# Reordering the entry of the block-product stage: two more banks, block sums on another engine, a convolution in another place

## The chip, the cores and the metric

The kernel runs on one core of one Trainium2 chip. The metric is device microseconds of one launch. A core has TensorE (PE, matrix products), VectorE (DVE), ScalarE (ACT), GpSimd (POOL) and SyncE (SP), which here only issues transfers. Each runs its own instruction stream in order; they meet through semaphores. Products land in PSUM, eight banks of 128 x 512 fp32.

## What is computed

One layer of a hybrid decoder for a prompt of 1024 tokens and a sample group of 8 x 8 tokens, with the same weights. The part that matters here is the first projection and the gated short convolution:

```python
h = rms_norm(x, g_pre_mix)
cb, cc, ch, q, k, v, ga, gb = jnp.split(h @ w_in, IN_SPLITS, axis=-1)
conv_u, conv_state = causal_dwconv(cc * ch, conv_prev, w_conv_a)
y_a = (cb * conv_u) @ w_a
...
o = stick_breaking(q, k_all, v_all, sb_bias)
y_b = o @ w_b
merged = jax.nn.sigmoid(ga) * y_a + jax.nn.sigmoid(gb) * y_b
x = x + rms_norm(merged @ w_o, g_post_mix)
```

Attention, the output projection, a convolutional FFN and a per-layer embedding follow.

## The kernel before

Every fp32 operand is split into a high part (rounded copy, made by ACT) and a low part (the rest, made by DVE), and each product is three PE matmuls: high x high, high x low, low x high. A job is one 128-column slice of `w_in` against all 1088 tokens, in three groups of 384, 384 and 320 tokens.

**The opening** (0 to 51 us). Two jobs (`cc` and `ch`, channels 0 to 127) are six units: group 0 of job 0, group 0 of job 1, group 1 of job 0, and so on. Unit u writes bank u % 2. `open_unit` (L3142) makes PE wait, through `drained` (L3127), until the bank of unit u - 2 has been read: for job 0 by ACT (`conv_in`, L1424, which copies into `uc`), for job 1 by DVE (`conv_by`, L2287, which multiplies into `uc`). Banks 2 to 7 hold the turned input blocks meanwhile; bank 7 also takes the turned convolution weights, which ACT copies out (semaphore `a_m`).

**The block-product stage** (51 to 230 us). Seven pairs of 128-column slices of `w_in` (`WIDE_PAIRS`: gate, c, b, c, c, b, gate, numbered 0 to 6) are multiplied by the prompt as 2 x 2 blocks with seven block products of 12 matmuls each instead of eight (a Strassen-Winograd scheme), plus a product "S" of 16 narrower matmuls for the sample tokens. PE runs them per pair in the order of `wide_order`: "1S267543" for pair 0, "162S7543" for the others. The scheme needs sums of blocks:

- of the input, once: four raw sums `wsraw` S1 to S4 (`raw_sum`, L2345, on DVE, 128 x 2048 elements per operation), their high part by ACT (`sum_high`, L1478) and their low part by DVE (`sum_low`, L2333). Product 6 reads S2, 5 reads S1, 7 reads S3, 3 reads S4.
- of the weights, for each pair: `wtb` and `wtc` (`wide_sums`, L1200, four POOL operations of 128 x 512), their high and low parts by `wide_b` and `wide_c` on ACT and DVE; `wide_h` does the plain weights.
- of the results: ACT takes a snapshot of bank "1" (`wu2`) before product 2 is added into that bank; DVE adds u2 (after 6), u3 (after 7), c22 (after 5), the sample sum, c21 (after 4) and c12 (after 3). Product 4 waits for u3, product 3 for c22.

After a c pair (1, 3, 4) POOL multiplies `uc` by the other factor (`wide_times`, L1221, semaphore `g_wm`), and DVE runs the depthwise convolution over it (`convolve`, L2298) in the loop turn of the next pair. ACT's next copy into `uc` (`wide_c11`, L1511) waits for that convolution (`d_c`). The semaphores `a_wh` and `d_wl` count high and low parts; the tables `W_HIGH` and `W_LOW` (L145 to L148) turn a part's name into its count, so their order must be that of the code on ACT and DVE. SP loads the next pair's weights into the one buffer `wraw0` when the current pair's last low part from it is done.

**The attention part** (230 us on) runs four head pairs (`pair`, L1569, L2431, L3346). POOL clears `aas`, `vn`, `aasp` and `qpad` before it (`g_const` reaches 6), and ACT waits for that and for eight small output stores (`so_out`) ahead of the first head pair. `new_rows` (L3363) turns key and value rows on PE, between the pieces of fill jobs.

Of the kernel before, what the change touches and what calls it, by code (L numbers as in the profile page):

```python
# [144 lines left out]
W_HIGH = wide_table([("h0", 0), ("h1", 0), ("S2",), ("b", 0), ("S1",), ("c", 0), ("S3",), ("S4",)]  # L145
                    + [x for n in range(1, NW) for x in (("h0", n), ("b", n), ("c", n), ("h1", n))])
W_LOW = wide_table([("h0", 0), ("h1", 0), ("S2",), ("b", 0), ("S1",), ("c", 0), ("S3",), ("S4",)]
# [98 lines left out]
def build(nc, inp, out, gate_spill, x1_spill, x2_spill, f_spill, c_spill):  # L246
    with ExitStack() as ctx:
# [906 lines left out]
        def _(pool):  # L1154
# [45 lines left out]
            def wide_sums(n):  # L1200

                w = wraw0
                pool.wait_ge(w_in_, 64 * (n + 1))
                if n:
                    pool.wait_ge(d_wl, W_LOW["c", n - 1])
                else:
                    pool.wait_ge(p_x0, 2 * NBK)
                minus(wtc[:, 0, :, :], w[:, 1, 0:KH, :], w[:, 0, 0:KH, :]).then_inc(g_wt, 1)
                pool.wait_ge(g_wt, 4 * n + 1)
                minus(wtb[:, 1, :, :], w[:, 1, KH:KD, :], wtc[:, 0, :, :]).then_inc(g_wt, 1)  # L1210
                minus(wtb[:, 0, :, :], w[:, 1, KH:KD, :], w[:, 1, 0:KH, :]).then_inc(g_wt, 1)
                pool.wait_ge(g_wt, 4 * n + 2)
                minus(wtc[:, 1, :, :], w[:, 0, KH:KD, :], wtb[:, 1, :, :]).then_inc(g_wt, 1)
# [21 lines left out]
            wide_sums(0)  # L1235
# [91 lines left out]
        def _(act):  # L1327
# [96 lines left out]
            def conv_in(gr):  # L1424

                act.wait_ge(p_unit, 2 * gr + 1)
                b = banks[0][:, 0:GROUPS[gr][1]]
                for d, cols in padded(uc, gr):
                    ins = s_.activation(d, like(b[:, cols], d), ACT.Copy)
                ins.then_inc(a_u, 1)  # L1430
# [53 lines left out]
            wide_h(0, 1)  # L1484
            conv_in(2)
            sum_high(1, 2)
            wide_b(0)
            sum_high(0, 1)
            wide_c(0)

# [39 lines left out]
            for n in range(NW):  # L1530
# [8 lines left out]
                if n == 0:  # L1539
                    sum_high(2, 3)  # L1540
# [25 lines left out]
            act.wait_ge(g_const, 6)  # L1566
            act.wait_ge(so_out, soo.at())

            def pair(c, last=False):  # L1569
# [75 lines left out]

                for n in range(SLOTS):
# [539 lines left out]
        def _(dve):  # L2186
# [100 lines left out]
            def conv_by(gr):  # L2287

                dve.wait_ge(p_unit, ENDS[0] + 1 if gr == NG - 1 else 2 * gr + 2)
                dve.wait_ge(a_u, gr + 1)  # L2290
                b = banks[1][:, 0:GROUPS[gr][1]]
                for d, cols in padded(uc, gr):
                    ins = v.tensor_tensor(d, like(b[:, cols], d), d, ALU.mult)
                ins.then_inc(d_u, 1)
# [53 lines left out]

            then(raw_sum(0, block_of(xh, 0, 1), block_of(xh, KH, 1), ALU.add, ALU.add, block_of(xl, 0, 1)))
# [4 lines left out]
            wide_h(0, 0)  # L2354
            wide_h(0, 1)
            sum_low(1)
            wide_b(0)
# [3 lines left out]
            dve.wait_ge(d_ws, 2)  # L2361
            raw_sum(2, block_of(xh, KH, 1), wsraw[1][:, :, :], ALU.subtract, ALU.add, block_of(xl, KH, 1)).then_inc(d_ws, 1)
# [32 lines left out]
            for n in range(NW):  # L2395
# [8 lines left out]
                dve.wait_ge(d_wq, W_SUM["u2", n])  # L2404
                summed(n, "u3", "7", wu3[:, :], wu2[:, :])
                if n > 1 and n - 1 in CONV_AFTER:
                    dve.wait_ge(g_wm, W_TIMES[n - 1])
                    convolve(CONV_AFTER[n - 1])
                if n + 1 < NW:
                    wide_h(n + 1, 0)  # L2410
# [650 lines left out]
        def _(pe):  # L3061
# [80 lines left out]
            def open_unit(j, gr):  # L3142
                u = job_unit(j, gr)
                if u >= 2 and u not in (6, 7):
                    drained(u - 2)
                unit.step()
# [132 lines left out]
            def wide_sample(n):  # L3279
# [4 lines left out]
                else:  # L3284
                    pe.wait_ge(a_wp, 1)
                    pe.wait_ge(a_u, NG)
# [6 lines left out]
            def wide_fold(n):  # L3293
# [3 lines left out]
                else:  # L3297
                    pe.wait_ge(d_u, NG)
# [47 lines left out]
            def pair(c):  # L3346
# [149 lines left out]
                for n in range(SLOTS):  # L3496
# [8 lines left out]
                    if n == 0:  # L3505
                        new_rows(vT, 0)
# [402 lines left out]
```

## Time and profile before

| | |
|---|---|
| median of 3 runs | 1743.21 us (1741.01 to 1745.79) |
| the profiled execution | 1742.35 us |
| its span in the trace | 1740.4 us |
| mean granted PE clock | 0.986 of full |

The page gives busy time per engine over the span. The rows below come from views of the trace: the timeline (each instruction with its start and length in us, the engine, the line in the kernel, output <- inputs, shapes; in square brackets how long the engine stood idle before it and who released it), the busy time by stretches, and the page. PE's granted clock is a share of 2.4 GHz, so that 0.50 is 1.2 GHz.

### The profile page before, as it was taken

To read this page: it belongs to the slowest core of one execution; us is meant where nothing else is said; L and a number is where in the kernel's file an instruction comes from. 1 tells how busy PE (TensorE), PEld (TensorE's weight loads), DVE (VectorE), ACT (ScalarE), POOL (GpSimd) and SP (SyncE) were. 2 spreads that over 40 slices of the span, in tenths; PEclk is the share of its full clock that TensorE was granted. 3 is DMA by queue.
4 is the path that set the end of the run, shared out by engine and by line. 5 is a ranking of instruction groups with operands and counts; after the bars stand their busy time and mean duration, and the time that the engine had idled before them with its cause. 6 is when DMAs were issued, how large, how long until landed. Compare 5 with 4: busy or idle time off the path is not lost.

```text
span 1740.4 us, 25950 instructions
## 1 busy us (share of the span) xinstructions
PE 1668.9 (96%) x8709; PEld 1426.1 (82%) x8709; DVE 1189.1 (68%) x1674; ACT 832.0 (48%) x1433; POOL 371.3 (21%) x295
## 2 busy tenths in 40 slices
PE   8799888998999989999999999999999999999998
PEld 7578688797797887998888888888888888888886
DVE  8854633725627447654878888888888789777566
ACT  7321225645546456313654444444444544456665
POOL 3334300000000000000106666666666100000100
PEclk9799999999999999999999999999999999999999
DMA  4122153123131131444313222222221773244343
GB/s 165 31 68 75 35 166 109 39 73 97 34 102 60 49 101 35 143 163 146 122 61 112 77 76 76 76 76 83 82 76 38 238 258 127 75 145 161 120 138 115
DMA packets 178314, 174.98 MB, mean 101 GB/s; under 512 B 17423, under 2 KB 144235, under 8 KB 178220
## 3 DMA queue, kind: packets, MB, share of 16 engines
q1 hardware_dynamic: 167274, 168.87, 29.8%
q10 hardware_dynamic: 10946, 4.91, 1.0%
q8 instruction: 52, 0.85, 0.2%
q14 instruction: 42, 0.34, 0.1%
HBM read 131.89 MB, written 41.84 MB: 100 GB/s over the span
## 4 chain that ended last, share of the span: by engine, by line
PE 65%; DVE 3%; ACT 1%; issue 1%; DMA 0%; POOL 0%; ACTq 0%; SPq 0%; DVEq 0%; POOLq 0%
PE pair L3582 10%; PE pair L3642 8%; PE pair L3644 8%; PE pair L3643 8%; PE pair L3780 4%; PE pair L3781 4%; PE pair L3782 4%; PE pair L3651 2%; PE pair L3107 2%; PE pair L3083 2%; PE pair L3084 2%; PE pair L3082 2%; PE pair L3151 1%; PE pair L3153 1%; PE pair L3152 1%; DVE left L2502 1%
## 5 line engine op out<-in xcount | busy, mean ns | idle before, releaser
L3151 PE MATMUL pair<-xh,wh 128*128 128x384 f32 (+1 forms) x600 | 211.4, 352 | 9.9 <-DVE qs L2442 4.5
L3153 PE MATMUL pair<-xh,wl 128*128 128x384 f32 (+1 forms) x600 | 200.0, 333 | 0.0
L3152 PE MATMUL pair<-xl,wh 128*128 128x384 f32 (+1 forms) x600 | 199.7, 333 | 0.0
L1195 POOL TENSOR_TENSOR hn<-hn 128x512 f32<-128x512 f32 x4 | 5.2, 1289 | 659.5 <-DVE hn L2636 659.5
L3151 PEld LDWEIGHTS pair<-xh,wh 128*128 128x128 f32 x600 | 116.5, 194 | 14.5 <-DVE qs L2442 4.9
L3780 PE MATMUL pair<-woph,foph 128*128 128x512 f32 x308 | 120.5, 391 | 0.0
L3782 PE MATMUL pair<-woph,fopl 128*128 128x512 f32 x308 | 119.9, 389 | 0.0
L3781 PE MATMUL pair<-wopl,foph 128*128 128x512 f32 x308 | 119.9, 389 | 0.0
L3152 PEld LDWEIGHTS pair<-xl,wh 128*128 128x128 f32 x600 | 116.4, 194 | 0.0
L3153 PEld LDWEIGHTS pair<-xh,wl 128*128 128x128 f32 x600 | 115.9, 193 | 0.0
L2199 DVE TENSOR_TENSOR wl<-raw,wh 128x1024 fp32r<-128x1024 f32 x33 | 40.4, 1225 | 71.5 <-ACT wh L1353 71.3
L1660 ACT ACTIVATE keep<-pair,bias 128x512 f32<-128x512 f32 (+4 forms) x100 | 58.0, 580 | 61.3 <-DVE pair L2491 33.7
L2000 ACT ACTIVATE foph<-f 128x512 fp32r<-128x512 f32 x77 | 48.3, 628 | 76.8 <-PE pair L3782 73.4
L3780 PEld LDWEIGHTS pair<-woph,foph 128*128 128x128 f32 x308 | 57.8, 188 | 12.2 <-issue 0.2
L3782 PEld LDWEIGHTS pair<-woph,fopl 128*128 128x128 f32 x308 | 57.8, 188 | 12.1
L3781 PEld LDWEIGHTS pair<-wopl,foph 128*128 128x128 f32 x308 | 57.8, 188 | 11.8
L3642 PE MATMUL pair<-bh,tch 128*128 128x512 f32 x168 | 67.4, 401 | 0.0
L3107 PE MATMUL pair<-ident,beta 128*128 128x128 f32 x300 | 51.9, 282 | 14.7 <-DVE beta L2508 14.2
L3644 PE MATMUL pair<-bh,tcl 128*128 128x512 f32 x168 | 65.7, 391 | 0.0
L3642 PE MATMUL pair<-bh,adh 128*128 128x512 f32 x168 | 65.5, 390 | 0.2 <-DVE adl L2645 0.2
L3643 PE MATMUL pair<-bl,tch 128*128 128x512 f32 x168 | 65.5, 390 | 0.0
L3644 PE MATMUL pair<-bh,adl 128*128 128x512 f32 x168 | 65.4, 389 | 0.0
(525 smaller groups left out, 4872.7 us busy)
## 6 DMA issues: line engine op xcount, KB each, us to landing
rawp<-in_w_up SPq DMA_DIRECT2D x88, 256.0 KB, 3.7
wd<-in_w_down SPq DMA_DIRECT2D x55, 256.0 KB, 3.0
raw<-in_w_in SPq DMA_DIRECT2D x52, 256.0 KB, 3.4
f_spill<-cv SPq DMA_DIRECT2D x22, 552.0 KB, 2.8
f<-f_spill SPq DMA_DIRECT2D x44, 256.0 KB, 5.7
gat<-gate_spill SPq DMA_DIRECT2D x16, 544.0 KB, 4.4
x_spill<-x SPq DMA_DIRECT2D x16, 512.0 KB, 2.9
wraw<-in_w_in SPq DMA_DIRECT2D x28, 256.0 KB, 3.8
```

Source lines behind the costliest of these rows:

```text
L1660: s_.activation(keep[n % 2][:, 4 * P - w:4 * P], b, ACT.Sigmoid, scale=-SCALE, bias=bias2[:, h + 2:h + 3] if n != SAMPLE else bias2[:, 5:6 ...
L3107: return t_.transpose(b, src, ident[0:rows, 0:rows])
L3151: t_.matmul(b, h, xhi, start=(k == 0), stop=False, skip_group_check=True)
L3152: t_.matmul(b, h, xlo, start=False, stop=False, skip_group_check=True)
L3153: ins = t_.matmul(b, l, xhi, start=False, stop=(k == KD - 1), skip_group_check=True)
L3582: ins = t_.matmul(o[:, 512 * c:512 * c + 512], x, w(t, c), start=first and i == 0, stop=last and i == 2, skip_group_check=True)
L3642: t_.matmul(o, w, x, start=n in "1675" and k == 0, stop=False, skip_group_check=True)
L3643: t_.matmul(o, w, xlow, start=False, stop=False, skip_group_check=True)
L3644: ins = t_.matmul(o, wlow, x, start=False, stop=k == KH - 1, skip_group_check=True)
L3780: t_.matmul(o, xh_[:, cols], w[0][:, :], start=n in (0, 2, 3, 5) and k == 0, stop=False, skip_group_check=True)
L3781: t_.matmul(o, xh_[:, cols], w[1][:, :], start=False, stop=False, skip_group_check=True)
L3782: ins = t_.matmul(o, xl_[:, cols], w[0][:, :], start=False, stop=k == KF - 1, skip_group_check=True)
```

## The change

- The last two opening units (group 2 of both jobs) write banks 6 and 7 instead of 0 and 1. PE doesn't wait for `drained` there, but for `a_m`; ACT and DVE read those banks for group 2, and products S and the fold wait for one group less.
- The first pair's block sums of the weights move from POOL (`wide_sums(0)`) to DVE (`block_sums`), at the head of DVE's sums. The first plain weights' low parts follow right behind, ahead of the input sums.
- On DVE the block half b of the weights comes before S2's low part, the third raw sum before `conv_by(2)`; on ACT b comes before `conv_in(2)` and S2, and the high part of S3 goes ahead of the snapshot of product 1. The two tables follow.
- `convolve` for pairs 1, 3, 4 runs between the sums u2 and u3 of the next pair instead of behind u3. For pair 0 it stays.
- ACT's wait for the cleared buffers and the small stores moves from ahead of the first head pair to ahead of its score loop.
- The first value rows of a head pair are turned after the first piece of the fill job instead of after the second.

```diff
@@ -142,9 +142,9 @@
     return {"g": (6 * CW, 2 * m + h), "c": (((CW, 2 * CW)[h]), m), "b": (0, m + h)}[kind]
 
 
-W_HIGH = wide_table([("h0", 0), ("h1", 0), ("S2",), ("b", 0), ("S1",), ("c", 0), ("S3",), ("S4",)]
+W_HIGH = wide_table([("h0", 0), ("h1", 0), ("b", 0), ("S2",), ("S1",), ("c", 0), ("S3",), ("S4",)]
                     + [x for n in range(1, NW) for x in (("h0", n), ("b", n), ("c", n), ("h1", n))])
-W_LOW = wide_table([("h0", 0), ("h1", 0), ("S2",), ("b", 0), ("S1",), ("c", 0), ("S3",), ("S4",)]
+W_LOW = wide_table([("h0", 0), ("h1", 0), ("b", 0), ("S2",), ("S1",), ("c", 0), ("S3",), ("S4",)]
                    + [x for n in range(1, NW) for x in (("h0", n), ("b", n), ("c", n), ("h1", n))])
 W_SUM = wide_table([x for n in range(NW) for x in (("u2", n), ("u3", n), ("c22", n), ("smp", n), ("c21", n), ("c12", n))])
 
@@ -1201,10 +1201,7 @@
 
                 w = wraw0
                 pool.wait_ge(w_in_, 64 * (n + 1))
-                if n:
-                    pool.wait_ge(d_wl, W_LOW["c", n - 1])
-                else:
-                    pool.wait_ge(p_x0, 2 * NBK)
+                pool.wait_ge(d_wl, W_LOW["c", n - 1])
                 minus(wtc[:, 0, :, :], w[:, 1, 0:KH, :], w[:, 0, 0:KH, :]).then_inc(g_wt, 1)
                 pool.wait_ge(g_wt, 4 * n + 1)
                 minus(wtb[:, 1, :, :], w[:, 1, KH:KD, :], wtc[:, 0, :, :]).then_inc(g_wt, 1)
@@ -1232,7 +1229,6 @@
                         times(conv_out[i][:, :], wide0[i][:, :])
                     times(conv_s[:, :, :], wide_s[:, :, :]).then_inc(g_wm, 1)
 
-            wide_sums(0)
             for n in range(NW):
                 if n + 1 < NW:
                     wide_sums(n + 1)
@@ -1424,7 +1420,7 @@
             def conv_in(gr):
 
                 act.wait_ge(p_unit, 2 * gr + 1)
-                b = banks[0][:, 0:GROUPS[gr][1]]
+                b = banks[6 if gr == NG - 1 else 0][:, 0:GROUPS[gr][1]]
                 for d, cols in padded(uc, gr):
                     ins = s_.activation(d, like(b[:, cols], d), ACT.Copy)
                 ins.then_inc(a_u, 1)
@@ -1482,11 +1478,12 @@
 
             wide_h(0, 0)
             wide_h(0, 1)
+            wide_b(0)
             conv_in(2)
             sum_high(1, 2)
-            wide_b(0)
             sum_high(0, 1)
             wide_c(0)
+            sum_high(2, 3)
 
             def copied(ins):
                 ins.then_inc(a_wc, 1)
@@ -1536,8 +1533,6 @@
                 if n:
                     act.wait_ge(d_wq, W_SUM["c12", n - 1])
                 copied(s_.activation(wu2[:, :], wide_bank["1"], ACT.Copy))
-                if n == 0:
-                    sum_high(2, 3)
                 wide_sc(n)
                 if n == 0:
                     sum_high(3, 4)
@@ -1563,8 +1558,6 @@
                         act.dma_start(cs_o[:, c * P:c * P + P], sot[18 * c + 2:18 * c + 18, :]).then_inc(so_out, 16)
                     soo.step(128)
             gated(NW - 1, "c12", wide0[1][:, 0:HALF])
-            act.wait_ge(g_const, 6)
-            act.wait_ge(so_out, soo.at())
 
             def pair(c, last=False):
 
@@ -1643,6 +1636,9 @@
                     act.wait_ge(stg_out[gr], stn[gr].at(16 * job_))
                     s_.activation(stg[gr][:, 0:GROUPS[gr][1]], b, ACT.Sigmoid).then_inc(a_gt, 1)
 
+                if c == 0:
+                    act.wait_ge(g_const, 6)
+                    act.wait_ge(so_out, soo.at())
                 for n in range(SLOTS):
                     if n < NSTEP:
                         w, masked = step_shape(n)
@@ -2288,7 +2284,7 @@
 
                 dve.wait_ge(p_unit, ENDS[0] + 1 if gr == NG - 1 else 2 * gr + 2)
                 dve.wait_ge(a_u, gr + 1)
-                b = banks[1][:, 0:GROUPS[gr][1]]
+                b = banks[7 if gr == NG - 1 else 1][:, 0:GROUPS[gr][1]]
                 for d, cols in padded(uc, gr):
                     ins = v.tensor_tensor(d, like(b[:, cols], d), d, ALU.mult)
                 ins.then_inc(d_u, 1)
@@ -2346,20 +2342,33 @@
                 then(v.tensor_tensor(wsraw[q][:, :, :], first, second, op))
                 return v.tensor_tensor(wsraw[q][:, :, :], wsraw[q][:, :, :], by, to)
 
+            def block_sums():
+
+                w = wraw0
+                dve.wait_ge(w_in_, 64)
+                dve.wait_ge(p_x0, 2 * NBK)
+                v.tensor_tensor(wtc[:, 0, :, :], w[:, 1, 0:KH, :], w[:, 0, 0:KH, :], ALU.subtract).then_inc(g_wt, 1)
+                dve.wait_ge(g_wt, 1)
+                v.tensor_tensor(wtb[:, 1, :, :], w[:, 1, KH:KD, :], wtc[:, 0, :, :], ALU.subtract).then_inc(g_wt, 1)
+                v.tensor_tensor(wtb[:, 0, :, :], w[:, 1, KH:KD, :], w[:, 1, 0:KH, :], ALU.subtract).then_inc(g_wt, 1)
+                dve.wait_ge(g_wt, 2)
+                v.tensor_tensor(wtc[:, 1, :, :], w[:, 0, KH:KD, :], wtb[:, 1, :, :], ALU.subtract).then_inc(g_wt, 1)
+
+            block_sums()
+            wide_h(0, 0)
+            wide_h(0, 1)
             then(raw_sum(0, block_of(xh, 0, 1), block_of(xh, KH, 1), ALU.add, ALU.add, block_of(xl, 0, 1)))
             v.tensor_tensor(wsraw[0][:, :, :], wsraw[0][:, :, :], block_of(xl, KH, 1), ALU.add).then_inc(d_ws, 1)
             conv_by(1)
             dve.wait_ge(d_ws, 1)
             raw_sum(1, wsraw[0][:, :, :], block_of(xh, 0, 0), ALU.subtract, ALU.subtract, block_of(xl, 0, 0)).then_inc(d_ws, 1)
-            wide_h(0, 0)
-            wide_h(0, 1)
+            wide_b(0)
             sum_low(1)
-            wide_b(0)
+            dve.wait_ge(d_ws, 2)
+            raw_sum(2, block_of(xh, KH, 1), wsraw[1][:, :, :], ALU.subtract, ALU.add, block_of(xl, KH, 1)).then_inc(d_ws, 1)
             conv_by(2)
             sum_low(0)
             wide_c(0)
-            dve.wait_ge(d_ws, 2)
-            raw_sum(2, block_of(xh, KH, 1), wsraw[1][:, :, :], ALU.subtract, ALU.add, block_of(xl, KH, 1)).then_inc(d_ws, 1)
             sum_low(2)
             then(v.tensor_tensor(wsraw[3][:, :, :], block_of(xh, KH, 0), wsraw[1][:, :, :], ALU.subtract))
             v.tensor_tensor(wsraw[3][:, :, :], wsraw[3][:, :, :], block_of(xl, KH, 0), ALU.add).then_inc(d_ws, 1)
@@ -2401,11 +2410,11 @@
                 v.tensor_tensor(wu2[:, :], wide_bank["6"], wu2[:, :], ALU.add).then_inc(d_wq, 1)
                 if n == 0:
                     sum_low(3)
-                dve.wait_ge(d_wq, W_SUM["u2", n])
-                summed(n, "u3", "7", wu3[:, :], wu2[:, :])
                 if n > 1 and n - 1 in CONV_AFTER:
                     dve.wait_ge(g_wm, W_TIMES[n - 1])
                     convolve(CONV_AFTER[n - 1])
+                dve.wait_ge(d_wq, W_SUM["u2", n])
+                summed(n, "u3", "7", wu3[:, :], wu2[:, :])
                 if n + 1 < NW:
                     wide_h(n + 1, 0)
                 wide_free(n)
@@ -3141,9 +3150,13 @@
 
             def open_unit(j, gr):
                 u = job_unit(j, gr)
+                unit.step()
+                if u == NG * FIRST_JOBS - 1:
+                    pe.wait_ge(a_m, 1)
+                if NG * FIRST_JOBS - 2 <= u < NG * FIRST_JOBS:
+                    return banks[6 + j][:, 0:GROUPS[gr][1]]
                 if u >= 2 and u not in (6, 7):
                     drained(u - 2)
-                unit.step()
                 return banks[u % 2][:, 0:GROUPS[gr][1]]
 
             def step(b, j, gr, k):
@@ -3283,7 +3296,7 @@
                     pe.wait_ge(a_wc, W_COPY["sc", n - 1])
                 else:
                     pe.wait_ge(a_wp, 1)
-                    pe.wait_ge(a_u, NG)
+                    pe.wait_ge(a_u, NG - 1)
                 for k in range(KD):
                     for t in (wadh, wadl):
                         ins = t_.matmul(wide_s_bank, wpack[:, k, :], t[:, :, k, :], start=k == 0 and t is wadh,
@@ -3295,7 +3308,7 @@
                 if n:
                     pe.wait_ge(d_wq, W_SUM["smp", n - 1])
                 else:
-                    pe.wait_ge(d_u, NG)
+                    pe.wait_ge(d_u, NG - 1)
                 pe.wait_ge(a_wc, W_COPY["sc", n])
                 for h in range(2):
                     ins = turned(wide_f_bank[:, P * h:P * h + P], wsb[:, h, :])
@@ -3502,8 +3515,8 @@
                         weights_turned(n - 2)
                     for i in range(first_piece(n), first_piece(n + 1)):
                         piece(*divmod(i, KD))
-                    if n == 0:
-                        new_rows(vT, 0)
+                        if i == 0:
+                            new_rows(vT, 0)
                     if n == STATE_SLOT:
                         sample_new()
                         sample_pages()
```

## Rows read from the trace of the kernel before

**Rows 1.** The page's busy time of each engine (share of the span), with its instructions.

```profile
PE 1668.9 (96%) x8709; PEld 1426.1 (82%) x8709; DVE 1189.1 (68%) x1674; ACT 832.0 (48%) x1433; POOL 371.3 (21%) x295
```

**Rows 2.** Timeline of PE at the entry: start, length, engine, line, operation; idle before and releaser.

```profile
45.05 0.64 PE L3151 MATMUL pair<-xh,wh 128*128 128x320 f32 x1 [4.38 <-DVE uc L2293]
...
69.34 0.79 PE L3274 MATMUL pair<-ws2h,wtbh 128*128 128x512 f32 x1 [7.27 <-DVE ws2l L2331]
...
80.79 0.50 PE L3274 MATMUL pair<-xh,wtch 128*128 128x512 f32 x1 [3.05 <-DVE wu L2370]
```

**Rows 3.** PE by stretches: from:to, length, busy (instructions), granted clock, DMA share, GB/s.

```profile
45.00:51.20 6.20, 6.15 (x24) 0.54 0.00 0
...
69.30:74.60 5.30, 5.26 (x12) 0.50 0.01 3
...
80.80:85.20 4.40, 4.40 (x12) 0.61 0.00 0
...
179.85:185.00 5.15, 5.15 (x14) 0.61 0.00 0
```

**Rows 4.** Timeline of PE: the first matmuls of products 1, S and 2.

```profile
51.32 0.50 PE L3274 MATMUL pair<-xh,wadh 128*128 128x512 f32 x1
...
54.16 0.28 PE L3289 MATMUL pair<-wadh,wpack 128*128 128x256 f32 x1
...
56.31 0.50 PE L3274 MATMUL pair<-xh,wadh 128*128 128x512 f32 x1
```

**Rows 5.** Timeline of DVE at the entry.

```profile
35.31 2.64 DVE L2346 TENSOR_TENSOR wsr<-xh 128x2048 f32<-128x2048 f32 x1
...
47.84 2.29 DVE L2347 TENSOR_TENSOR wsr<-wsr,xl 128x2048 f32<-128x2048 f32 x1
...
50.05 2.35 DVE L2331 TENSOR_TENSOR wadl<-wraw,wadh 128x1024 fp32r<-128x1024 f32 x2
...
66.04 3.25 DVE L2331 TENSOR_TENSOR ws2l<-wsr,ws2h 128x2048 fp32r<-128x2048 f32 x1 [1.98 <-ACT ws2h L1451]
...
87.73 0.17 DVE L2301 COPY uc<-cwt 128x16 f32<-128x16 f32 x1
...
91.95 0.68 DVE L2370 TENSOR_TENSOR wide<-pair,wu 128x512 f32<-128x512 f32 x1
```

**Rows 6.** Timeline of ACT at the entry: high part of S2, snapshot of product 1.

```profile
50.16 1.92 ACT L1451 ACTIVATE ws1h<-wsr 128x2048 fp32r<-128x2048 f32 x1 [8.96 <-DVE wsr L2347]
...
55.68 0.57 ACT L1538 ACTIVATE wu<-pair 128x512 f32<-128x512 f32 x1
```

**Rows 7.** Timelines of SP and POOL: loading and summing the weights of pair 1.

```profile
59.64 2.02 SPq L796 DMA_DIRECT2D wraw<-in_w_in  x4
...
65.88 1.26 POOL L1190 TENSOR_TENSOR wtc<-wraw 128x512 f32<-128x512 f32 x1 [20.22 <-DMA wraw<-in_w_in]
```

**Rows 8.** Timeline of PE: the pauses in the later pairs, all of them before product 3.

```profile
131.00 0.50 PE L3274 MATMUL pair<-ws3h,wadh 128*128 128x512 f32 x1 [2.54 <-DVE wide L2370]
...
179.85 0.80 PE L3274 MATMUL pair<-ws3h,wadh 128*128 128x512 f32 x1 [5.65 <-DVE wide L2370]
...
205.59 0.50 PE L3274 MATMUL pair<-ws3h,wadh 128*128 128x512 f32 x1 [2.34 <-DVE wide L2370]
```

**Rows 9.** Timelines of POOL, DVE and ACT in pair 4.

```profile
162.31 0.32 POOL L1216 TENSOR_TENSOR uc<-uc,wide_s 128x64 f32<-128x64 f32 x1
...
168.62 0.69 DVE L2370 TENSOR_TENSOR wu<-pair,wu 128x512 f32<-128x512 f32 x1 [6.76 <-PE pair L3276]
...
176.39 0.60 ACT L1518 ACTIVATE uc<-pair 128x512 f32<-128x512 f32 x1 [10.21 <-DVE conv_s L2273]
```

**Rows 10.** Timelines of SP, ACT and PE in the first head pair.

```profile
235.46 0.94 SPq L739 DMA_DIRECT2D raw<-in_w_in  x2
...
239.34 1.06 ACT L1353 ACTIVATE wh<-raw 128x1024 fp32r<-128x1024 f32 x1 [6.15 <-DMA raw<-in_w_in]
...
281.92 0.52 PE L3107 MATMUL pair<-ident,vT 128*128 128x128 f32 x3 [1.81 <-ACT vn L1367]
```

## The prediction

> **What bounds the kernel now.** I read first the busy time per engine: TensorE (PE) is busy 1668.9 of 1740.4 us [rows 1], so a change pays only by what PE idles or runs slowly. Then I took PE's waits and its timeline over the part the diff touches. At the entry of the block-product stage (products in the order 1, S, 2, 6, 7, 5, 4, 3 for the first pair) PE stands three times: 4.38 us before the last opening unit, until DVE has emptied the bank (the copy it waits for is queued behind three 128x2048 operations that begin at 35.31, [rows 5]); 7.27 us before product "7", until the low part of the third input sum is there; 3.05 us before "4", until DVE's sum u3 is there [rows 2]. Each pause is followed by a stretch at PE's lower level: granted clock 0.54, 0.50, 0.61 [rows 3], where 0.50 is 1.2 GHz and 1.00 is 2.4 GHz. A stretch loses its length times (1 - clock): 6.20 x 0.46 = 2.9 us, 5.30 x 0.50 = 2.7 us, 4.40 x 0.39 = 1.7 us. At full clock a product of 12 matmuls takes 54.16 - 51.32 = 2.84 us, and S, with the short gap behind it, 56.31 - 54.16 = 2.1 us, of which 1.9 us are matmuls [rows 4]. The later pairs have three more pauses, 2.54, 5.65 and 2.34 us, all before product "3", all on DVE [rows 8]; only the 5.65 us one is followed by a slow stretch, 5.15 us at 0.61, 2.0 us lost [rows 3].
>
> Who is late in each case? In the entry it is DVE: from 35 to 87 us it hardly stops. Its 128x2048 operations take 2.29 us alone, and 3.25 us while GpSimd (POOL), which adds the block sums of the weights, runs beside it, as from 65.88 us on [rows 5, 7]. In pair 4 DVE computes u3 at 168.62 and then a whole convolution; ACT's copy into the buffer the convolution reads waits 10.21 us, to 176.39, DVE's next half weight waits for ACT, and only behind it comes c22, which product "3" needs [rows 8, 9].
>
> **The change, part by part.**
>
> (a) *Two more banks.* The last two opening units go to banks 6 and 7. PE no longer waits for DVE there; its new wait, for ACT's copy of the convolution weights, is met long before, since ACT does that copy ahead of those of the last input blocks. The unit that began at 45.05 begins at 45.05 - 4.38 = 40.7 [rows 2] and runs at full clock: 6.20 us at 0.54 [rows 3] become 3.4 us, to 44.0 or so, where before it ended at 51.2. What is late next is the first weight's low half.
>
> (b) *First block sums on DVE, ahead of the input sums.* Four 128x512 operations. The trace has no such operation with both inputs in SBUF on DVE; the nearest row, 128x512 with one input in PSUM, is 0.68 us [rows 5]; back to back an operation costs about 0.1 us less than its length (two of 1.22 take 2.35, same rows), so 0.6. I take 2.6 us for four with one wait; the ends are 2.4 us and, at POOL's uncontended pace (1.26 us, [rows 7]), 4 x 1.3 = 5.2 us. In return DVE's first input sums lose POOL beside them (3.25 to 2.29 us each, three of them, plus part of a fourth), about 3 us. The Trainium skill, page "VectorE: DVE Perf Modes", section on the TRN2 errata, gives (N+151)/0.96 ns for such an add, 0.69 us at 512 elements; an estimate from it is 2.8 us, which would shift the entry by 0.2 us.
>
> (c) *The new order, walked through.* DVE: sums 35.35 to 37.95 (the start of its first input sum before, [rows 5]); low halves of the weight (2.35 us for two) to 40.25. PE takes product "1" from 44.0 to 46.85 and S to 48.8 without a pause. But product "2" waits for ACT's snapshot of "1", and on ACT that snapshot now stands behind the high part of the third input sum, which had stood after it. Before, it was taken at 55.68, right after the weight's last high part [rows 6]. So I follow DVE to that sum: first sum, three operations at 2.3, to 47.1; conv_by 0.5; second sum 4.6, to 52.2; block half 1.1; wait for ACT's 1.92 us high part [rows 6], low part from 54.2 to 56.4; third sum 4.6, to 61.0. ACT: high part 61.1 to 63.0, snapshot 0.57 [rows 6], to 63.55. PE stands from 48.8 to 63.6, 14.8 us in one piece. It starts cold: I charge one stretch as after the 7.27 us pause, so "2" takes 5.1 us to 68.7, then "6" to 71.5, and "7" (its low part is there at 67.0) to 74.35, the fold and "5" to 77.3. The old "5" ended at 77.7: four and a half us of bank wait and cold opening were turned into waiting, not into time.
> The wait of product "6" counts one table entry fewer than the low part of the second sum, but the snapshot's place behind the third sum covers it on DVE's own order.
> The gain is in what follows. DVE: conv_by 0.5, low part 2.2, block half 1.1, low part 2.2, fourth sum 4.6, to 71.6; ACT 1.9; low part 73.6 to 76.85, charged 3.25 us because POOL's sums of pair 1, run beside it: their weights are loaded once the last block half's low part is done, issue at 59.64 and first sum at 65.88 before [rows 7], now 64.9 and 71.1; u3 to 77.5. PE begins "4" at 77.55 instead of 80.79 and at full clock instead of 1.7 us slower: 3.2 + 1.7 = **4.9 us**. DVE, not PE, then carries it on: from u3 at 77.5 a weight half (1.5 beside POOL), c22 0.6, a block half 1.1, the sample sum 0.4, c21 0.6, the last block half 1.2 and the convolution of 4.2 us (87.73 to 91.95, [rows 5]) end at 87.1 against 91.95, so product "2" of pair 1 starts 4.8 us sooner. I take **4.8 us** for the entry. Bounds: 5.2 us for (b) leaves 2.2; no POOL beside the low part and a shorter cold stretch give 6.0.
>
> (d) *Convolution between u2 and u3 in pairs 2, 4, 5.* Nothing is added; 4.2 us (up to 7 with POOL beside) move into the time where DVE waits for product "7". In pair 4 u2 is there by then, and the moved convolution needs POOL's multiply, which ends at 162.31 + 0.32 = 162.63 [rows 9]; it runs to about 166.9; u3 could not start before 168.62 in any case. Slack 1.7 us, and 2.8 more before "4" would stand. POOL's multiply is the one new wait in front of u3, c22 and the next weight halves, all queued behind it on DVE. c22 then follows product "5" directly, so the three pauses go: 2.54 + 5.65 + 2.34 = 10.5 us, and the slow stretch after the middle one, 1.9 us of the 2.0 computed: **12.4 us**. Next in line is the low block half of the next pair; by this schedule it comes over 5 us before product "6" uses it. If the cover failed in pair 4 alone, 7.5 of the 12.4 us would stay.
>
> (e) *The later wait for cleared buffers and the state rows.* ACT's next operation starts at 239.34, released by a weight load issued by SP from 235.46, its second half 0.5 us later, and loads land in about 3.4 us, so it is the load that decides [rows 10]. The wait moved away hides nothing: **0 us**, at most 0.4 us if the load is at its fastest.
>
> (f) *The value rows turned one step (three matmuls, 0.5 us) earlier.* PE stands at 281.92 for ACT's copy, which ACT starts late by its own order, not for lack of rows [rows 10]. The step only changes sides with the pause: 0 us, between -0.5 and +0.5 in each of four pairs.
>
> **Sum.** 4.8 + 12.4 + 0 = 17.2 us. The profiled execution took 1742.35 us for a span of 1740.4; the span becomes 1723.2. The median of the runs, 1743.21, lies 0.9 above the profiled one, so I predict 1743.2 - 17.2 = **1726.0 us**.
>
> **Rivals.** (1) *The entry gives nothing.* The pause before "2" takes the place of the three old ones, and if DVE is 2 to 3 us later (dearer block sums, POOL beside more than one operation) or the cold stretch is longer than 5 us, the 4.8 us vanish. For it: the path from 35 to 77 us is DVE's alone, and it has no slack. Against: PE and DVE each have nearly the work they had. Time 1743.2 - 12.4 = 1730.8.
> (2) *The moved convolutions still hold u3 or c22.* If the pause of pair 4 survives: 4.8 + 4.9 = 9.7 us, 1733.5. Against it: 1.7 + 2.8 us of slack.
> (3) *More than forecast*: entry 6.0, the load wait 0.4, and 0.5 us in each of four pairs: 20.8 us, 1722.4.
> (4) *Slower: the clock doesn't come back.* PE's longest pause in this part is 7.27 us; the new one is twice that. In the rows PE is at full level again about 5 us after it resumes [rows 3]. PE at 1.2 GHz loses half of the elapsed time, so 17.2 us are used up by 34 us more at the low level; with 50 us more, 25 us are lost, and the time is 1751. Nothing in the trace shows such a stretch. The Trainium skill, page "TensorE: Matmul & The Clock Gate", section "Seeing it yourself", reports a throttle stuck low for over 50 us on this kind of chip; by that report this rival would be real, but no row here bears it out.
>
> **Chances.** Forecast 0.62; rival 1 0.16; rival 2 0.07; rival 3 0.09; rival 4 0.03; that parts cancel and nothing is left 0.03. The forecast's own range is 1723 to 1729 (bounds of the entry, 2.2 to 6.0, and noise of a us). With rivals 1 and 3 mostly inside, and rival 2 at the edge, the range is 1721 to 1734. A measurement of this kernel tells 0.3%, 5.2 us, from nothing: faster 0.94, the same 0.03, slower 0.03.
>
> **What would show it.** (a): no pause at 40.5, opening ends near 44. (b): four DVE operations of 0.7 us after 35.3, none on POOL before 70. (c): one pause of 13 to 16 us before product "2", released by ACT's snapshot; under 1 us before "4"; the second pair's "2" at about 89. (d): no pause before any "3" of pairs 2, 4, 5, full clock from 90 us to the end of the stage. (e), (f): the pauses of 4.5 and 1.8 us as before, only earlier. The prediction is wrong if the snapshot comes later than 66 us, if the slow stretch after it is over 7 us, or if a new wait for POOL's multiply stands before u3.

## The result, and the profile after

The changed kernel takes 1720.2 us (median of 4 runs, 1718.7 to 1722.9), the kernel before 1744.1 us: ratio 0.9867, interval 0.9847 to 0.9886, so 23 us or 1.3% faster. Forecast were 1726.0 us and 17.2 us of gain, with a range of 1721 to 1734. The sign came out, and so did the mechanisms of the entry and of the convolution; the gain is a third larger, and the time lies just below the range.

PE's waits over the whole span of the changed kernel (engine, line, waited for: us in total, times, longest), where [rows 2] and [rows 8] stood before:

```profile
engine line waited for: us in total, times, longest us
PE pair L3116 <- DVE beta L2517: 15.4, 28, 1.4
PE pair L3287 <- ACT wu L1535: 15.1, 2, 14.5
PE pair L3444 <- ACT beta L1658: 5.8, 8, 1.4
PE pair L3116 <- ACT vn L1363: 5.2, 4, 1.4
PE pair L3164 <- DVE qs L2451: 4.5, 1, 4.5
...
PE pair L3287 <- DVE wu L2379: 0.4, 1, 0.4
PE pair L3164 <- DVE kl L2451: 0.3, 1, 0.3
```

The pauses on DVE's `wide`, `ws2l` and `uc` are gone. One of 14.46 us before product 2 has come, released by ACT's snapshot, and 0.38 us are left before product 4. The same in PE's timeline, with DVE's entry (its rows answer to [rows 5]) and POOL's first operation (to [rows 7]):

```profile
63.41 0.80 PE L3287 MATMUL pair<-xh,wadh 128*128 128x512 f32 x1 [14.46 <-ACT wu L1535]
76.79 0.50 PE L3287 MATMUL pair<-xh,wtch 128*128 128x512 f32 x1 [0.38 <-DVE wu L2379]
```

```profile
35.41 0.67 DVE L2350 TENSOR_TENSOR wtc<-wraw 128x512 f32<-128x512 f32 x1
...
37.33 0.69 DVE L2355 TENSOR_TENSOR wtc<-wraw,wtb 128x512 f32<-128x512 f32 x1
37.94 2.35 DVE L2327 TENSOR_TENSOR wadl<-wraw,wadh 128x1024 fp32r<-128x1024 f32 x2
40.21 2.28 DVE L2342 TENSOR_TENSOR wsr<-xh 128x2048 f32<-128x2048 f32 x1
...
54.11 2.29 DVE L2327 TENSOR_TENSOR ws1l<-wsr,ws1h 128x2048 fp32r<-128x2048 f32 x1 [0.84 <-ACT ws1h L1447]
...
73.44 2.69 DVE L2327 TENSOR_TENSOR ws3l<-wsr,ws3h 128x2048 fp32r<-128x2048 f32 x1 [1.39 <-ACT ws3h L1447]
76.05 0.68 DVE L2379 TENSOR_TENSOR wu<-pair,wu 128x512 f32<-128x512 f32 x1
...
86.72 0.69 DVE L2379 TENSOR_TENSOR wide<-pair,wu 128x512 f32<-128x512 f32 x1
```

```profile
70.89 1.72 POOL L1190 TENSOR_TENSOR wtc<-wraw 128x512 f32<-128x512 f32 x1 [59.35 <-DMA wraw<-in_w_in]
```

DVE has no gap of 1 us between 35.4 and 72 us: it is the engine that times the entry. c12, the last row, comes at 86.72 instead of 91.95. PE by stretches (columns as in [rows 3], with every engine's busy time):

```profile
63.40:68.50 5.10, 5.09 (x16) 4.09 (x17) 5.10 (x4) 0.23 (x1) 0.00 (x0) 0.67 0.47 136
68.50:76.40 7.90, 7.90 (x36) 6.17 (x34) 6.48 (x5) 3.35 (x3) 5.43 (x3) 1.00 0.24 78
76.80:90.00 13.20, 12.55 (x54) 10.10 (x55) 12.32 (x19) 5.71 (x9) 2.70 (x2) 1.00 0.20 67
90.00:224.39 134.39, 129.78 (x634) 109.79 (x632) 73.94 (x102) 36.31 (x54) 54.08 (x36) 1.00 0.24 75
```

There is one slow stretch after the long pause and then full clock to the end of the stage; before there was one in the opening and three more in the stage.

Where the 22.8 us between the two spans lie, by the same instruction in both timelines: product 2 of pair 1 starts 5.2 us sooner (88.61 against 93.84). At product 3 of pair 2 it is 7.9 us, of pair 4 13.8 and, the slow stretch behind it included, 15.8, of pair 5 18.3 us. The last q unit of the first head pair starts at 224.39 against 242.87 (18.5). From there the lead grows in three steps of 1.5 us, to 20.5, 22.1 and 23.6 us, in head pairs 1, 2 and 3; by 1000 us it is 22.8 again. At each step the kernel before has a slow stretch behind its pause before the second value rows, and the changed kernel has none. Before:

```profile
282.80:286.20 3.40, 3.40 (x14) 3.40 (x14) 2.34 (x7) 0.79 (x3) 0.00 (x0) 0.50 0.42 124
398.90:402.30 3.40, 3.40 (x13) 3.29 (x13) 2.83 (x8) 0.63 (x2) 0.00 (x0) 0.50 0.89 263
514.90:518.30 3.40, 3.40 (x14) 3.27 (x13) 2.82 (x8) 0.63 (x2) 0.00 (x0) 0.50 0.67 198
```

So some 5 us of this profiled execution are gained behind the stage, where I had forecast nothing.

### The profile page after: what moved, and what is told of

Its sections match the earlier page's. It is cut to its first block, busy times and chain, and to the rows that moved or that the text cites. A ratio compares the mean times of both kernels' runs of the same rounds, so it can differ in the third digit from the quotient of the medians.

```text
span 1717.6 us, 25950 instructions
## 1 busy us (share of the span) xinstructions
PE 1657.8 (97%) x8709; PEld 1416.9 (82%) x8709; DVE 1184.6 (69%) x1678; ACT 832.3 (48%) x1433; POOL 360.6 (21%) x291
## 4 chain that ended last, share of the span: by engine, by line
PE 61%; DVE 2%; issue 0%; ACT 0%; DMA 0%; POOL 0%; SPq 0%; DVEq 0%; POOLq 0%; ACTq 0%
PE pair L3595 10%; PE pair L3655 8%; PE pair L3656 8%; PE pair L3657 8%; PE pair L3793 4%; PE pair L3795 4%; PE pair L3794 4%; PE pair L3664 2%; PE pair L3116 2%; PE pair L3093 2%; PE pair L3091 2%; PE pair L3092 2%; PE pair L3603 1%; DVE left L2511 1%; PE pair L3779 1%; PE pair L3778 1%
## 5 line engine op out<-in xcount | busy, mean ns | idle before, releaser
L3116 PE MATMUL pair<-ident,beta 128*128 128x128 f32 x300 | 51.9, 282 | 15.8 <-DVE beta L2517 15.4
```

The costliest lines, as they stand in the source:

```text
L3116: return t_.transpose(b, src, ident[0:rows, 0:rows])
```

## Experiments

Ratios are to the kernel before on the same chip, with a 95% interval; a gain in us is 1 minus the ratio, times 1743 us. Experiments 1, 3, 4 and 6 take the change apart; 2, 5, 7 and 8 fill a pause or move it, to see what sets a time; 9 tries the banks alone; 10 and 11 move what is left in the first head pair.

**1. The convolution's place alone**

```diff
-                dve.wait_ge(d_wq, W_SUM["u2", n])
-                summed(n, "u3", "7", wu3[:, :], wu2[:, :])
                 if n > 1 and n - 1 in CONV_AFTER:
                     dve.wait_ge(g_wm, W_TIMES[n - 1])
                     convolve(CONV_AFTER[n - 1])
+                dve.wait_ge(d_wq, W_SUM["u2", n])
+                summed(n, "u3", "7", wu3[:, :], wu2[:, :])
```

> The kernel before with only the convolution of pairs 2, 4 and 5 moved ahead of u3. Theory: the pauses of 2.54, 5.65 and 2.34 us and the slow stretch behind the second go, 12.4 to 13 us, 1731 us, ratio 0.9925. Rival: the multiply of POOL holds it in pair 4 and half of the gain stays away, 6 us.

Measured: 1727.0 us, 0.9910 (0.9897 to 0.9924), 15.7 us (13.2 to 18.0). All three pauses are gone. The theory's 12.4 to 13 us are too little; the rival is excluded.

**2. The same pauses, filled.** PE issues transposes of the identity before it waits.

```diff
                     elif what == "3":
+                        for _ in range({2: 20, 4: 48, 5: 18}.get(n, 0)):
+                            turned(banks[0][:, 3 * P:4 * P], ident[:, :])
                         pe.wait_ge(d_wq, W_SUM["c22", n])
```

> The kernel before with 20, 48 and 18 transposes of the identity, issued by PE into an unused part of a bank, in its pauses of 2.54, 5.65 and 2.34 us before product 3 of pairs 2, 4 and 5. Nothing is moved; the pauses stay, the clock doesn't fall. Theory: the slow stretches behind these pauses cost more than the one profiled execution of before shows (1.9 us behind the 5.65 us pause alone); over executions 3.5 to 4.5 us, because the two short pauses are followed by a slow stretch in some of them, ratio 0.9975 to 0.998. Rival, that the convolution's extra gain has another source and the prediction's 1.9 us is right: ratio 0.999.

Measured: 1738.0 us, 0.9977 (0.9966 to 0.9988), 4.0 us (2.1 to 5.9), with product 3 released as late as before; in pair 4 it starts at 179.28 against 179.85, and at full clock where before it had 0.61:

```profile
179.28 0.50 PE L3274 MATMUL pair<-ws3h,wadh 128*128 128x512 f32 x1 [0.61 <-DVE wide L2370]
```

```profile
180.00:185.00 5.00, 5.00 (x24) 4.12 (x23) 4.54 (x7) 1.06 (x1) 1.89 (x1) 1.00 0.01 3
```

So clock is what is gained. That all 4.0 us belong to these three pauses is not shown. By the profiled executions only 2.1 us are gained up to the last q unit (240.82 against 242.87); 5.1 us more come in the four head pairs, where this execution has none of the three slow stretches of the kernel before, although nothing was changed there. Whether such a stretch comes differs between executions, in the head pairs as in the stage.

This shows when the stretch behind the pause of pair 2 is read in other kernels that have the pause. First the kernel with the rows alone (experiment 4), then the filled attention pause (5), then the entry alone (3), the wait alone (6) and the banks alone (9), each 5 us from the start of product 3:

```profile
131.40:136.40 5.00, 4.96 (x15) 3.94 (x16) 3.43 (x6) 0.26 (x1) 0.00 (x0) 0.66 0.00 0
```

```profile
130.40:135.40 5.00, 4.91 (x15) 3.87 (x15) 3.77 (x7) 0.55 (x1) 0.00 (x0) 0.66 0.00 0
```

```profile
131.00:136.00 5.00, 4.94 (x15) 3.91 (x16) 3.64 (x7) 0.45 (x1) 0.00 (x0) 0.66 0.00 0
```

```profile
131.70:136.70 5.00, 4.97 (x22) 4.10 (x23) 4.54 (x7) 1.06 (x1) 1.13 (x1) 1.00 0.00 0
```

```profile
131.60:136.60 5.00, 4.98 (x22) 4.13 (x23) 4.54 (x7) 1.06 (x1) 1.15 (x1) 1.00 0.01 3
```

The pause is 2.1 to 2.8 us in all of them and in the kernel before [rows 8]; the clock behind it falls in three of six executions (0.66 of full, 1.7 us lost) and stays in the other three. Behind the 5.5 to 5.8 us pause of pair 4 it is low in all six, for 4.0 to 5.7 us, and behind the 2.1 to 2.9 us pause of pair 5 in one of six. The average of the six is an estimate of what the clock costs behind the three pauses: 2.4 + 0.9 + 0.2 = 3.5 us, against the 1.9 us of the one execution that I had. With the pauses' 10.5 us that makes 14.0, within the interval of experiment 1. The Trainium skill, page "TensorE: Matmul & The Clock Gate", section "What's actually happening", says that the chip watches activity in a window that runs free of the kernel's start, so that the number of slow matmuls differs from run to run. That the clock behind one and the same pause differs between executions, 3 of 6, fits this; no row shows the window.

**3. The entry alone**: the changed kernel without the edits of 1, 4 and 6.

> The kernel before with the two banks, the block sums on DVE and the new order of the entry, and none of the other edits. Theory: product 2 of pair 1 starts 5.3 us sooner and that reaches the end, 1739 us, ratio 0.997. Rival: the entry gives nothing by itself, since the 14.5 us pause takes the place of the three old ones, and the time the changed kernel shows at 90 us is taken back later: 0 us.

Measured: 1736.3 us, 0.9964 (0.9951 to 0.9977), 6.3 us (4.0 to 8.5). The rival is excluded. (The profiled execution, at 1747.0 us, is the longest of the nine, so its rows are used here only for single pauses and stretches.)

**4. The value rows alone**

```diff
                         piece(*divmod(i, KD))
-                    if n == 0:
-                        new_rows(vT, 0)
+                        if i == 0:
+                            new_rows(vT, 0)
```

> The kernel before with only the value rows turned one piece earlier. Theory: this step, predicted at 0 us, is where most of the missing gain is. In the changed kernel the pause before the second value rows (1.81 us) is split by a piece into 0.26 and 1.43 us, and the stretch at 1.2 GHz behind it, seen in the first head pair from 283.5 to 286.1 us, is gone; per head pair 1.0 to 1.3 us, in sum 4 to 5 us, ratio 0.997 to 0.998. Rival A (the step of the prediction): 0 us. Rival B: the gain behind 260 us comes from another edit, the later wait of ACT; then this run shows the 1.8 us pauses or the slow stretches as before and 0 us.

Measured: 1740.8 us, 0.9990 (0.9978 to 1.0002), 1.7 us with an interval that reaches zero (-0.3 to 3.8). In the profiled execution none of the four head pairs has a slow stretch behind the second value rows; in the first one, 4.3 us are at clock 0.60 before and at 1.00 here, behind pauses of 1.81 and 1.33 us. Before, then with the rows alone:

```profile
282.00:286.30 4.30, 4.30 (x20) 4.27 (x21) 2.44 (x7) 1.12 (x3) 0.00 (x0) 0.60 0.54 161
```

```profile
286.00:290.30 4.30, 3.96 (x28) 3.66 (x29) 2.72 (x8) 1.66 (x5) 0.00 (x0) 1.00 0.32 91
```

**5. The same pause, filled**: the kernel before with

```diff
+                    if n == 0:
+                        if c:
+                            pe.wait_ge(a_wT, att.at())
+                        for _ in range(14):
+                            turned(banks[5][:, 0:P], ident[:, :])
                     if n < NG - 1:
                         new_rows(vT, n + 1)
```

> The kernel before, with 14 transposes of the identity into a bank that is free, issued by PE in front of the second value rows of each head pair: nothing is moved, and PE has something to do in the pause. Theory that the clock is what is gained: the slow stretch behind the pause goes, 1.0 to 1.3 us in those head pairs in which before has one, 3 to 4 us in sum, though the second rows start as late as before. Rival, that the gain is the earlier rows themselves: 0 us or slower by up to 1 us.

Measured: 1738.7 us, 0.9981 (0.9970 to 0.9993), 3.3 us (1.2 to 5.2). Nothing was moved, so what is gained is clock: the slow stretches behind these pauses cost some 3 us. That the step of experiment 4 gains through the same stretches is an argument from the traces, as its own timing is too coarse. Six kernels here keep the pause of 1.71 to 1.84 us (before and experiments 1, 2, 3, 6 and 9), and a slow stretch follows in 14 of their 24 head pairs. Five have the step (the changed kernel and experiments 4, 7, 8 and 11), and one follows in 3 of 20, each time in the first head pair. At 1.5 us a stretch that is an estimate of 2.7 us for the step.

**6. The later wait alone**: ACT's `g_const` and `so_out` waits moved as in the change, nothing else.

> The kernel before with only ACT's wait for the cleared buffers and the small stores moved behind the projections of the first head pair. Theory (the step of the prediction): the weight load lands last, so ACT's copy of it starts as late after SP's issue as before, the pause of 4.5 us stays, and the time is the same within the measurement, 0 us. Rival: the small stores land later than the load; then the copy starts up to 2 us sooner and the pause shrinks.

Measured: 1742.6 us, 1.0005 (0.9990 to 1.0021): no effect that can be told. ACT's row (answers to [rows 10]) names the load again:

```profile
240.41 1.06 ACT L1353 ACTIVATE wh<-raw 128x1024 fp32r<-128x1024 f32 x1 [6.12 <-DMA raw<-in_w_in]
```

The parts add up: 15.7 + 6.3 + 1.7 - 0.9 = 22.8 us, against 23 for the whole. Each part is uncertain by 2 to 3 us, so this agrees better than it had to.

**7. The snapshot back in its old place**, on the changed kernel:

```diff
             wide_c(0)
-            sum_high(2, 3)
...
                 copied(s_.activation(wu2[:, :], wide_bank["1"], ACT.Copy))
+                if n == 0:
+                    sum_high(2, 3)
...
-                        pe.wait_ge(d_wl, W_LOW["b", n])
+                        pe.wait_ge(d_wl, W_LOW["b", n] if n else W_LOW["S2",])
```

> The changed kernel with ACT's snapshot of product 1 back in its old place, ahead of the high part of the third input sum, and product 6 waiting for the second sum's low part by its own count. Products 2 and 6 then run by about 59 us instead of 71 us, and the 14.5 us pause of PE becomes one of some 8 us before product 7. Theory that DVE's own row of operations sets the entry: u3, product 4 and product 2 of pair 1 start at the same time within 0.5 us, and the total stays, 0 us. Rival that the snapshot's place costs time: product 4 up to 1 us and the total 1 to 3 us sooner.

Measured: 1721.4 us, 0.9876 (0.9852 to 0.9900), no different from the changed kernel. PE's pauses:

```profile
57.70 0.80 PE L3288 MATMUL pair<-xh,wadh 128*128 128x512 f32 x1 [8.42 <-ACT wu L1534]
67.33 0.58 PE L3288 MATMUL pair<-ws2h,wtbh 128*128 128x512 f32 x1 [2.44 <-DVE ws2l L2328]
77.13 0.50 PE L3288 MATMUL pair<-xh,wtch 128*128 128x512 f32 x1 [2.20 <-DVE wu L2380]
90.18 0.50 PE L3288 MATMUL pair<-xh,wadh 128*128 128x512 f32 x1 [0.25 <-ACT wu L1534]
```

I was wrong on the shape: the snapshot is still behind two other high parts, so there are three pauses. 8.42 + 2.44 + 2.20 = 13.1 us against 14.5 + 0.4 in the changed kernel, and product 4 starts at 77.13 against 76.79: up to there where PE waits doesn't matter, DVE's row does. Behind it the expectation missed. A slow stretch follows the 2.20 us pause (77.1 to 82.1 at 0.66), and product 2 of pair 1 starts at 90.18, 1.6 us later than in the changed kernel:

```profile
88.61 0.50 PE L3287 MATMUL pair<-xh,wadh 128*128 128x512 f32 x1 [0.65 <-ACT wu L1535]
```

A difference of 1.6 us is too small for the timing to show.

**8. The long pause filled**: 120 transposes ahead of the wait for the snapshot, on the changed kernel.

```diff
                     elif what == "2":
+                        if n == 0:
+                            for _ in range(120):
+                                turned(banks[2][:, 0:P], ident[:, :])
                         pe.wait_ge(a_wc, W_COPY["snap", n])
```

> The changed kernel with 120 transposes of the identity into an unused bank, issued by PE in the 14.5 us pause before product 2, so that the clock stays at 2.4 GHz. Product 2 takes 2.8 instead of 5.1 us. Theory that DVE sets the entry: product 4 starts at the same time, total unchanged, 0 us. Rival that the slow stretch behind the long pause is a cost of the change: 2 to 2.5 us faster.

Measured: 1721.9 us, 0.9883 (0.9858 to 0.9907): not faster. Product 2 runs at full clock, and product 4 starts no sooner than in the changed kernel, 77.06 against 76.79; that speaks against the rival more firmly than the timing, whose interval ends just short of the rival's time. But PE is now early for product 4 and pauses 1.95 us there, this pause is followed by the slow stretch, and product 2 of pair 1 starts 1.5 us later, at 90.12:

```profile
77.06 0.50 PE L3287 MATMUL pair<-xh,wtch 128*128 128x512 f32 x1 [1.95 <-DVE wu L2379]
...
90.12 0.50 PE L3287 MATMUL pair<-xh,wadh 128*128 128x512 f32 x1 [0.24 <-ACT wu L1535]
```

```profile
63.60:69.00 5.40, 5.32 (x23) 4.43 (x24) 5.40 (x4) 0.30 (x2) 0.00 (x0) 1.00 0.46 129
77.00:82.00 5.00, 4.94 (x15) 3.89 (x16) 4.38 (x7) 1.45 (x3) 2.75 (x2) 0.66 0.01 3
```

So the slow stretch behind the long pause is free, but not one behind product 4's pause: there PE is no longer ahead of DVE.

**9. The banks alone**, on the kernel before: units 4 and 5 in banks 6 and 7, with the waits that go with them, and nothing else.

> The kernel before with only the two more banks for the opening. PE's 4.38 us pause and the slow opening unit go, and the unit ends at 44 instead of 51.2 us. Theory that DVE sets the entry: the first weight's low half comes at 51.3 us as before, so a pause of about 7 us stands there, and product 7 starts as before: 0 us. Rival: the earlier end of the opening reaches the end of the kernel, 2 to 5 us faster.

Measured: 1741.2 us, 0.9990 (0.9979 to 1.0002), nothing that can be told by time, where up to 3.7 us of the rival's 2 to 5 are within the interval. The trace speaks against the rival: the opening ends 7 us sooner, PE waits 7.15 us for the first weight's low half, and product 7 starts at 69.28 against 69.34:

```profile
51.20 0.80 PE L3278 MATMUL pair<-xh,wadh 128*128 128x512 f32 x1 [7.15 <-DVE wadl L2331]
69.28 0.79 PE L3278 MATMUL pair<-ws2h,wtbh 128*128 128x512 f32 x1 [5.75 <-DVE ws2l L2331]
```

**10. What is left in the first head pair**: on the changed kernel, q's first copies ahead of the wait for weights (ACT, and likewise DVE), and value rows 1 behind the first scores.

```diff
-                whi()
+                if c:
+                    whi()
                 for gr in range(NG):
+                    if c == 0 and gr == NG - 1:
+                        whi()
                     q_high(gr)
...
                         scores(n)
+                    if n == 1:
+                        new_rows(vT, 1)
...
-                    if n < NG - 1:
+                    if 0 < n < NG - 1:
                         new_rows(vT, n + 1)
```

> The changed kernel with two more edits in the first steps of the attention part. First: the first two copies of q, on ACT and DVE, go ahead of the work that waits for the next weights, in the first head pair. Theory: PE's pause of 4.5 us before the last q unit goes, a shorter one for those weights stands in its place (they land 1.3 us after the second q unit is done), and 2 to 5 us are gained. Second: the second value rows of each head pair are turned behind the first scores instead of ahead of them, so that 1.3 us of scores fill the pause of 1.3 to 1.4 us: theory 1 us each, 4 us in sum; rival: ACT's own order sets the scores' copies, and the pause appears a little later, 0 us. Together 1712 to 1715 us by the theories, 1718 to 1720 by the rivals.

Measured: 1721.6 us, 0.9882 (0.9861 to 0.9902): the rivals' time. The 4.5 us pause is gone and this one has come:

```profile
241.43 0.64 PE L3170 MATMUL pair<-xh,wh 128*128 128x320 f32 x1 [7.97 <-DVE kl L2454]
```

The value rows took the rival's way too: the four waits on `vn` (5.2 us) are gone, and those on `beta` before the scores have grown from eight of 5.8 us to twelve of 9.8 us. As for the new pause, in SP's queue the first head pair's third weights stand behind eight key loads and the four of `cout`:

```profile
218.80 8.12 SPq L840 DMA_DIRECT2D pk<-in_cache_k  x8
226.96 1.89 SPq L892 DMA_DIRECT2D cout<-c_spill  x4
228.96 1.00 SPq L739 DMA_DIRECT2D raw<-in_w_in  x2
```

**11. The same with another queue order**: value rows as in the change, q's first copies as in 10, and in SP's queue

```diff
-                load(in_job(c, 2))
+                if c:
+                    load(in_job(c, 2))
...
             keys(0, 0)
+            load(in_job(0, 2))
             keys(0, 1)
```

> The changed kernel with the first two copies of q ahead of the wait for the next weights, as in both_later_pauses, and in SP's queue the load of the third weights of the first head pair ahead of its second group of cached keys and of the reloading of the convolution's output. Theory: in both_later_pauses the 4.5 us pause before the last q unit was only exchanged for 8.0 us before the last k unit, because SP's row of small transfers ahead of that load set the landing; with the load ahead of them both pauses go but for 1 to 2 us, PE's last k unit starts 5 us sooner and the total is 1714 to 1716 us, ratio to before 0.984. Rival: the weights' landing is held by something else, and the time is that of the changed kernel, ratio 0.987.

Measured: 1714.6 us, 0.9839 (0.9823 to 0.9855), 28 us below the kernel before. Against the changed kernel's 0.9867 that is another 0.3%; the two intervals overlap, so timing alone doesn't settle it. The trace does: the weights leave 5.4 us sooner than in experiment 10, no wait on `qs` or `kl` is left, and the second value rows start at 259.08 against 262.96 in the changed kernel, although the entry ran 0.3 us later. At the end of this profiled execution 2.6 of these 3.9 us are left. The second block below is from PE's waits.

```profile
219.78 3.71 SPq L840 DMA_DIRECT2D pk<-in_cache_k  x4
223.61 0.94 SPq L739 DMA_DIRECT2D raw<-in_w_in  x2
```

```profile
PE pair L3295 <- ACT wu L1537: 15.1, 2, 14.5
...
PE pair L3124 <- ACT vn L1365: 5.2, 4, 1.4
PE pair L3124 <- DMA pk<-in_cache_k: 3.2, 3, 1.5
```

## Why the prediction was right or wrong

- **(a) banks.** Right: no pause, opening ends at 44.1. Alone nothing that can be told (9), as DVE's first weight half is late next.
- **(b) block sums.** 35.41 to 37.94, 2.5 us against 2.6. The figure from the page "VectorE: DVE Perf Modes" of the Trainium skill, section on the TRN2 errata, 0.69 us for one, is the measured length of one; from start to start it is 0.6.
- **(c) the new order.** The walk along DVE held within 0.2 us up to the snapshot: long pause 14.46 us (14.8 forecast), product 2 at 63.41 (63.6). Product 4 came at 76.79 (77.55), mostly because the 3.25 us charged beside POOL were 2.69, here and in all five other traces with this entry; the rows show POOL's second operation mostly in DVE's gap, but no run tests why. 5.2 us at pair 1 instead of 4.8; 6.3 (4.0 to 8.5) by time. That DVE times this part up to product 4 is shown by 7 and 8. "DVE, not PE, then carries it on" holds only with product 4 at full clock: both experiments have it slow and lose 1.5 us by pair 1. The stretch behind the long pause, charged 2.3 us on PE, took 1.6 (product 2 in 4.4 us instead of 2.8) and costs the kernel nothing.
- **(d) the convolution. The mechanism was right, one term was too small.** The pauses, 10.5 us, are gone. The term "the slow stretch after the middle one, 1.9 us" was read from one execution, in which the two short pauses happened to be followed by full clock and the middle one by the shortest slow stretch of the six. Over six traces it is 3.5 us, by filling 4.0 (2.1 to 5.9, part of it perhaps from the head pairs), and the whole part 15.7 (13.2 to 18.0) against 12.4.
- **(e) the wait.** Nothing measured against 0 forecast (6), to within 2 to 4 us; its row names the load, as forecast.
- **(f) value rows. Here a step failed.** "The step only changes sides with the pause" holds for the pause: 1.81 us became 0.26 and 1.43. But a slow stretch behind it becomes rarer, and that was charged nothing; no row that the forecast used shows the clock behind these pauses. In the two profiled executions it is the largest part of what was missed, three stretches or 5 us. By time it is 1.7 us (-0.3 to 3.8), and 3.3 (1.2 to 5.2) when the pause is filled. How much the two profiled executions differ there is partly luck: experiment 2 has no slow stretch there without the step.
- **The range.** Its lower end had 0.4 for the load and 2 us for the value rows, and nothing for clock in the stage, although [rows 3] showed a pause of 3.05 us with a slow stretch next to ones of 2.54 and 2.34 without. With 1.6 us more for (d) and 2.7 for (f), both estimates from above, the forecast would have been 1722 and the lower end 1717.
- **Rivals.** That the entry gives nothing is excluded by 3; that the moved convolution still holds u3 by 1; that the clock stays low by the stretch at 68.5, full again 5 us after PE resumed. The rival with more than forecast, 20.8 us, came nearest, but its surplus was to come from the entry, the load and the value rows' pauses, and not from the clock.

What stays open: 1.7 us of the convolution's gain over 10.5 + 3.5, how experiment 2's 4.0 us are shared between the stage and the head pairs, and whether the value rows' step is 0 or 4 us. None of these is larger than the intervals.

## What to carry to other kernels

Walk the engine that times a stretch operation by operation; a long pause of a faster engine, even one that restarts it cold, is free as long as that row sets the end; a slow stretch where it no longer does is paid in full. But price pauses of 1.8 to 3 us from more than one execution: the one that you see may have kept the clock by luck. And when a pause on a queue's load is removed, look at what that queue issues next before counting the gain: in experiment 10 it came back whole.

## What the hardware showed that was not expected

How often the clock was low within 2 us after a pause of PE, counted over the 13 traces from 34 us on: after 1.25 to 1.5 us in 4 of 100 cases, after 1.9 to 2.9 us in 11 of 19, after 3.0 to 3.2 us in 3 of 3, and after 4.0 us and more in 39 of 39, where it was back at 2.4 GHz 2.9 to 6.2 us after PE resumed, whether the pause was 4.0 or 14.5 us. After 1.71 to 1.84 us before the second value rows it was low in 14 of 24 cases, after pauses as long between 900 and 935 us in none of 13. Splitting that pause by 0.5 us of work left 3 of 20, and issuing 14 transposes in it 0 of 4, in one profiled execution.
